# Expert rounds of a streaming encoder layer: three prompt blocks dense, two blocks by gathered rows, weights rounded on ScalarE

## The reference

```python
# per block of 128 tokens, 8 heads, 16 picks each
s1 = einsum('nhd,kd->nhk', q[:, :, 0], sub_keys_1); s2 = ... sub_keys_2
v1, i1 = top_k(s1, 16); v2, i2 = top_k(s2, 16)
sc, ci = top_k(v1[..., :, None] + v2[..., None, :], 16)      # over 256 sums
experts = e1 * 128 + e2;  gate = softmax(sc)
act = gelu(einsum('nhkd,nd->nhk', u_table[experts], xt))
out = einsum('nhk,nhkd->nd', gate * act, v_table[experts])
y = layer_norm(alpha * h + out)
```

## Time and profile before

| | |
|---|---|
| Time, median of 3 runs | 5350.22 us (5346.51 to 5352.82) |
| Profiled execution's own span | 5353.8 us |
| PE busy / PE weight loads | 94% / 82% |
| DVE / POOL / ACT busy | 54% / 53% / 11% |
| DMA: moved, mean rate | 830.40 MB, 155 GB/s |
| DMA rate in the late groups | about 205 GB/s |

### The profile page before, as it was taken

One profiled execution on the slowest core, in us unless ns is written; L12 is line 12 of the kernel. 1 busy time (PEld: TensorE's weight loads), 2 busy tenths in 40 slices (PEclk: granted clock), 3 DMA queues, 4 the chain that ended last, 5 costly groups with the idle time before them and its releaser, 6 DMA issues.

```text
span 5353.8 us, 73076 instructions
## 1 busy us (share of the span) xinstructions
PE 5036.4 (94%) x26783; PEld 4365.9 (82%) x26783; DVE 2896.3 (54%) x4592; ACT 611.3 (11%) x1293; POOL 2825.4 (53%) x1256
## 2 busy tenths in 40 slices
PE   8999999999999898888889999999999999999996
PEld 8999888787899798676677777778888888888884
DVE  1000343444332389788776666666665656565666
ACT  1000222222210110122100000000000000000002
POOL 4444222222444333422276777677777777777772
PEclk9999999999999999999899999999999999999998
DMA  5222233121432211233366666665555555555552
GB/s 186 95 103 104 105 117 117 65 78 67 143 118 87 73 55 63 80 135 137 146 213 231 235 226 229 226 223 196 202 212 205 206 205 208 196 212 203 204 201 97
DMA packets 214977, 830.40 MB, mean 155 GB/s; under 512 B 17009, under 2 KB 93937, under 8 KB 132721
## 3 DMA queue, kind: packets, MB, share of 16 engines
q1 hardware_dynamic: 53280, 388.00, 20.4%
q0 software_dynamic: 36864, 268.45, 13.2%
q10 hardware_dynamic: 124752, 173.08, 9.5%
HBM read 757.51 MB, written 77.33 MB: 156 GB/s over the span
## 4 chain that ended last, share of the span: by engine, by line
PE 79%; DVE 11%; issue 5%; DMA 3%; ACT 1%; POOL 1%; ACTq 0%; DVEq 0%; POOLq 0%
PE banks L356 26%; PE banks L541 24%; PE banks L605 21%; PE banks L587 2%; PE banks L425 2%; PE banks L387 1%; DMA work<-in_u_rows,idx 1%; PE banks L395 1%; DVE work L1166 1%; PE banks L510 1%; DVE work L1014 1%; DVE work L1122 1%; DVE work L1130 1%; DVE work L1162 1%; DVE ww_lo L1242 1%
## 5 line engine op out<-in xcount | busy, mean ns | idle before, releaser
L305 POOL TENSOR_SCALAR w_hi<-w_raw 128x2048 fp32r<-128x2048 f32 x370 | 710.3, 1920 | 2099.1 <-PE banks L356 1357.4
L307 POOL TENSOR_TENSOR w_lo<-w_raw,w_hi 128x2048 fp32r<-128x2048 f32 x370 | 1761.4, 4760 | 30.9
L356 PE MATMUL banks<-mv_hi,w_hi 128*128 128x320 f32 x3648 | 870.1, 320 | 60.0 <-DVE mv_lo L967 36.6
L605 PE MATMUL banks<-ww_hi,w_hi 128*128 128x512 f32 x2048 | 808.2, 395 | 50.5 <-DVE ww_lo L1242 35.8
L356 PE MATMUL banks<-mv_lo,w_hi 128*128 128x320 f32 x3648 | 841.0, 312 | 0.0
L356 PE MATMUL banks<-mv_hi,w_lo 128*128 128x320 f32 x3648 | 840.5, 312 | 0.0
L541 PE MATMUL banks<-mv_hi,w_hi 128*128 128x512 f32 x2048 | 818.7, 400 | 11.7 <-POOL w_lo L307 5.9
L541 PE MATMUL banks<-mv_hi,w_lo 128*128 128x512 f32 x2048 | 806.0, 394 | 0.0
L541 PE MATMUL banks<-mv_lo,w_hi 128*128 128x512 f32 x2048 | 805.2, 393 | 0.0
L605 PE MATMUL banks<-ww_lo,w_hi 128*128 128x512 f32 x2048 | 804.7, 393 | 0.0
L605 PE MATMUL banks<-ww_hi,w_lo 128*128 128x512 f32 x2048 | 804.4, 393 | 0.0
(11 more groups left out here) (140 smaller groups left out, 4292.5 us busy)
## 6 DMA issues: line engine op xcount, KB each, us to landing
w_raw<-in_wstream SPq DMA_DIRECT2D x370, 1024.0 KB, 4.8
gate_matrix<-work ACTq DMA_DIRECT2D x16, 2048.0 KB, 6.5
work<-gate_matrix ACTq DMA_DIRECT2D x32, 1024.0 KB, 6.1
out_p<-work ACTq DMA_DIRECT2D x34, 320.0 KB, 2.2
work<-out_p ACTq DMA_DIRECT2D x34, 320.0 KB, 3.4
gate_scratch<-work ACTq DMA_DIRECT2D x32, 320.0 KB, 2.2
work<-gate_scratch ACTq DMA_DIRECT2D x16, 640.0 KB, 4.0
early_act<-work ACTq DMA_DIRECT2D x24, 256.0 KB, 3.9
```

Of the source, the lines that this page charges most:

```text
L305: pool.tensor_scalar(w_hi[s][:, :], raw[s][:, :], 1.0, 0.0, ALU.mult, ALU.add).then_inc(hi_done, 1)
L307: pool.tensor_tensor(w_lo[s][:, :], raw[s][:, :], w_hi[s][:, :].bitcast(f32), ALU.subtract) \
L356: last = pe.matmul(acc(dst)[:, h, :], a[s][:, P * k:P * k + P], b[:, k, HALF * h:HALF * h + HALF], start=(k == k_first and n == 0), stop=( ...
L605: last = pe.matmul(banks[:, d, :], a[v % 2][:, at:at + P], b[:, e, :], start=(e == 0 and n == 0), stop=(e == EG - 1 and n == 2))
```

## The change

- The 128 sample tokens and the first prompt block now are the first 256 columns (`N1`), the other three prompt blocks the last 384 (`N2`). Every phase for 640 tokens runs its two waves as 256 and 384 columns, with separate tiles for the operands; copies and subtractions by ScalarE and VectorE are made in two instructions.
- Dense expert work covers 384 columns (12 blocks of 32 tokens in the gate matrix). The gather path covers two blocks, one after the other: 128 steps on u and 128 on v for each. Row buffers: four, in place of two. Indices are fetched eight at a time.
- 16 early expert units in place of 24 (4 ahead of the G loop, 3 of them beside the selection), 4 mixed trips in place of 6, with all 128 gathers of the first block's u (3, 3, 3, 3, 4, 2, 2, 1, 3, 3, 3, 2 by unit), and 24 late groups in place of 20, with two gathers a unit.
- From the third unit of the mixed trips on ScalarE rounds `w_hi` (`split_high`, behind `unit_done`), and POOL only subtracts (`split_low`, for the unit two ahead). POOL's order in iteration n: gathers of n, then `split_low` of unit n+2.
- Gelu of the late groups is done in the PSUM bank; product and remainder read PSUM.
- The gathered blocks are normalized in token layout on VectorE (`bn_stats`), the first in the middle of the late groups, and stored by POOL.

```diff
-STEPS_G = 2 * PICKS // GROUPS
-MIXED_STEPS = [[0], [1], [2], [3], [4, 5], [6], [7], [8, 9], [10], [11, 12], [13], [14, 15]]
+STEPS_M = PICKS // EARLY
+STEPS_G = 16
+ROWS = 4
+MIXED = [3, 3, 3, 3, 4, 2, 2, 1, 3, 3, 3, 2]
+LATE_STEPS = [[2 * n, 2 * n + 1] for n in range(2 * EG)]
...
+            def low(s):
+                pool.tensor_tensor(w_lo[s][:, :], raw[s][:, :], w_hi[s][:, :].bitcast(f32), ALU.subtract) \
+                    .then_inc(split_done, 1)
+            def split_low(s, pair):
+                pool.wait_ge(hi_late, 2 * pair + s + 1 - SELF_SPLIT)
+                low(s)
...
+            def gather(table, trip, per, c, skip):
+                pool.wait_ge(rows_used, per * trip + c + skip + 1)
...
+                if c % 8 == 4:
+                    fetch_idx(per * trip + c + 4, (c + 4) // 8 % 2)
+                pool.indirect_dma_start(rows_t[c % ROWS], None, table,
+                                        bass.IndirectOffsetOnAxis(ap=idx2[:, c % 16:c % 16 + 1], axis=0)) \
+                    .then_inc(rows_in[c % ROWS], 16)
...
             with pool.Fori(0, EARLY) as i:
                 for n in range(3 * EG):
-                    split_next(n % 2, (U_PEER + N_EARLY) // 2 + 6 * i + n // 2)
                     for c in MIXED_STEPS[n]:
-                        gather(u_rows, 2 * i + c // STEPS_G, c % STEPS_G)
...
+                        gather(u_rows, i, STEPS_M, c, 0)
+                    split_low(n % 2, SELF_SPLIT // 2 + 6 * i + n // 2)
+            def late_group(table, g, n_units, skip):
+                for n in range(2 * EG):
+                    for c in LATE_STEPS[n]:
+                        gather(table, g - late + PICKS // STEPS_G, STEPS_G, c, skip)
+                    if n < n_units:
+                        split_low(n % 2, (U_PEER + 2) // 2 + EG * g + n // 2)
...
+                        last = pe.matmul(acc(dst, h), a[s][:, P * k:P * k + P], b[h][:, k, :],
...
+            def split_high(s, pair):
+                act.wait_ge(raw_full[s], 16 * pair + 16)
+                act.activation(w_hi[s][:, :], raw[s][:, :], ACT.Copy).then_inc(hi_late, 1)
...
+            def act_units(g, q, first, pair):
                 load_gates(g, q)
                 for e in range(EG):
                     act.wait_ge(unit_done, first + e + 1)
+                    if e < EG - 1:
+                        split_high(e % 2, pair + e // 2)
+                    act.activation(banks[:, e, 0:N2], banks[:, e, 0:N2], ACT.Gelu).then_inc(gelu_done, 1)
+                    if e == EG - 1:
+                        split_high(e % 2, pair + e // 2)
+                    high_part(q, e, 0, banks[:, e, 0:N2])
+            def out_unit(first, pair, v):
+                act.wait_ge(unit_done, first + v + 1)
+                split_high(v % 2, pair + v // 2)
...
+            def act_units(g, q, steps):
                 dve.wait_ge(g4_in, 16 * q + 16)
                 for e in range(EG):
+                    bank = banks[:, e, 0:N2]
+                    steps(e, 0, 1)
                     dve.wait_ge(gelu_done, 4 * g + e + 1)
+                    product(bank, e)
+                    if e < EG - 1:
+                        steps(e, 1)
+                    low_part(q, e, 0, bank)
+                    if e == EG - 1:
+                        steps(e, 1)
...
+                for v in range(EG):
+                    steps(EG + v)
+                    add_out(g, v, U_PEER + 8 * g + EG, sums)
```

More of the change, by code:

```diff
@@ L24 @@
 T = SEQ + DEC_B * DEC_T
+N1 = 2 * P
+N2 = T - N1
+WAVES = ((0, N1), (N1, N2))
 HALF = T // 2
@@ L315, in _, with fetch_idx @@
                 split(s, 0)
-            with pool.Fori(1, (U_PEER + N_EARLY) // 2) as i:
+            with pool.Fori(1, SELF_SPLIT // 2) as i:
                 for s in range(2):
                     split_next(s, i)
-            def gather(table, g, c, first=0):
-                idx = idx2[:, c % 2:c % 2 + 1]
-                pool.wait_ge(rows_used, STEPS_G * g + c + 1)
+            def fetch_idx(at, half):
+                pool.tensor_copy(idx2[:, 8 * half:8 * half + 8], idx_all[:, ds(at, 8)]).then_inc(idx2_ready, 1)
@@ L555, in tail_units, with natural @@
                         act_step(n % 2, k, n % 2)
+            def natural(blk):
+                for k in range(KT_N):
+                    for n, part in enumerate((mv_hi, mv_lo)):
+                        last = pe.matmul(nat[:, P * k:P * k + P], part[0][:, k, P * blk:P * blk + P].bitcast(f32), ident,
+                                         start=(n == 0), stop=(n == 1))
+                last.then_inc(nat_ready, 1)
             tail_units(0, TAIL_PICKS)
@@ L589, in _, with out_units @@
                     last.then_inc(g_full, 1)
[L590 removed]
+            pe.wait_ge(g_evac, 2 + N2 // 4)
             pe.wait_ge(gelu_done, N_EARLY)
[L594 to L600 removed]
+            def out_units(q, first, z):
                 def part(v, d, e):
@@ new lines, in late_group, with act_n_gelu_pass @@
+            def late_group(g, n_units):
+                first, pair = U_PEER + 8 * g, (U_PEER + 2) // 2 + 4 * g
+                act_units(g, g, first, pair)
+                for v in range(n_units):
+                    out_unit(first + EG, pair + 2, v)
+            def act_n_gelu_pass():
+                act.activation(act_n, act_n, ACT.Gelu).then_inc(act_n_gelu, 1)
+            late = 2 * EARLY
+            act.wait_ge(act_n_ready, 1)
+            act_n_gelu_pass()
+            with act.Fori(late, late + PASS_G) as g:
+                late_group(g, EG)
@@ new lines, in _, with steps, early_product @@
+            with dve.Fori(0, EARLY) as i:
+                own.enter(i, 1)
+                q, first = 2 * i + 1, U_PEER + N_EARLY + 12 * i + EG
+                def steps(n, lo=0, hi=None):
+                    for c in MIXED_STEPS[n][lo:hi]:
+                        gather_step("u", i, STEPS_M, c, 0, STEPS_M * i)
+                def early_product(e):
+                    dve.wait_ge(act_in[e % 2], 16 * (2 * i + e // 2 + 1))
+                    product(act_t[e % 2], e)
+                act_units(EARLY + i, 2 * i, steps)
@@ L1307, in _, with late_group, steps @@
[L1307 to L1315 removed]
+            def late_group(table, g, skip, col, sums=False):
+                def steps(n, lo=0, hi=None):
+                    for c in LATE_STEPS[n][lo:hi]:
+                        gather_step(table, g - late + PICKS // STEPS_G, STEPS_G, c, skip, col)
+                act_units(g, g, steps)
+                for v in range(EG):
+                    steps(EG + v)
+                    add_out(g, v, U_PEER + 8 * g + EG, sums)
@@ new lines, in weights, with norm_stats @@
+            def weights(blk):
+                own.wait()
+                own.done(dve.tensor_scalar(nat, nat, ALPHA, None, ALU.mult))
+                own.wait()
+                dve.sem_inc(act_n_ready, 1)
+                dve.wait_ge(act_n_gelu, blk + 1)
+                own.done(dve.tensor_tensor(act_n, act_n, gate_n[blk], ALU.mult))
+                own.wait()
+            def norm_stats(blk, used):
+                dve.wait_ge(rows_used, used)
+                for c in range(4):
+                    last = dve.bn_stats(bn_s[:, c, :], nat[:, 512 * c:512 * c + 512])
+                own.done(last)
+                own.wait()
+                own.done(dve.bn_aggr(bn_mv, ln_n[:, 0:24]))
+                own.wait()
+                dve.tensor_scalar(rstd_n, bn_mv[:, 1:2], 1.0, EPS, ALU.mult, ALU.add).then_inc(n_var, 1)
@@ new lines, in norm_out @@
+            def norm_out(blk, trip):
+                dve.wait_ge(n_std, blk + 1)
+                own.done(dve.reciprocal(rstd_n, rstd_n))
+                own.wait()
+                dve.wait_ge(rows_in[0], 16 * trip + 16)
+                own.done(dve.scalar_tensor_tensor(rows_t[0], nat, bn_mv[:, 0:1], rows_t[0], ALU.subtract, ALU.mult))
+                own.wait()
+                dve.wait_ge(rows_in[1], 16 * trip + 16)
+                dve.scalar_tensor_tensor(rows_t[1], rows_t[0], rstd_n, rows_t[1], ALU.mult, ALU.add).then_inc(n_ready, 1)
@@ new lines, in _ @@
+            late = 2 * EARLY
+            weights(0)
+            with dve.Fori(late, late + PASS_G) as g:
+                late_group("v", g, 0, STEPS_G * (g - late))
+            norm_stats(0, 2 * PICKS + ROWS)
+            norm_out(0, 2 * PICKS // ROWS)
+            dve.wait_ge(rows_in[2], 16 * (2 * PICKS // ROWS) + 16)
+            own.done(dve.tensor_copy(nat, rows_t[2]))
+            own.wait()
+            dve.wait_ge(n_ready, 1)
+            dve.sem_inc(rows_used, ROWS)
+            with dve.Fori(late + PASS_G, late + 2 * PASS_G) as g:
+                own.enter(g - late - PASS_G, 1)
+                late_group("u", g, ROWS, STEPS_G * (g - late - PASS_G))
+                own.leave(PASS_G)
```

463 lines of the change are left out of this document (246 added, 217 removed).

## The result

The changed kernel takes 5671.01 us (median of four runs, 5666.55 to 5673.1) where the one before takes 5349.73: 1.0595 times as long, interval 1.058 to 1.061. The profiled execution has a span of 5671.3 us.

The account below looks back on a forecast made before the run. PE was taken as the bound, 79% of the chain. 2551 us to the mixed trips, 740 for these, 2352 for 24 late groups, 30 block change, 52 end: 5725 of span, so 5720 us, 7% slower; range 5400 to 6000.

Parts of the forecast that it names:

- The order: POOL's queue in the late part: gather(n) stands behind a subtraction waiting for unit n-1, issuing 6.9 us after its end.
- Terms of a late group: Late group: four expert units 33.2 us, a stall 6.0, two output pairs 58.0, clock 1; 98 us, against 87 before.
- The pairs: Late group: from output unit n-1 done to n+1 done takes 29.0 us, where PE alone needs 16.6.
- 72.7 + 3L: Late group's time in us, with L the first gather's landing, if the second lands by the first's DVE step.
- Mixed trip: Each of four trips: output half pairs 122 us, expert units 45, stall 6, DVE's early work 12; 185 us, before 139.
- The rest: Outside mixed trips and late groups: 2551 us before the trips, G loop 268 of it; block change 30; end 52.
- PE's gain: 256 dense units lose 2.54 us of matmul time each, 650 us, but no longer on the path.
- Instructions: Late part: ScalarE's weight rounding takes 1.95 us; products and low parts reading PSUM take 0.5 us each.
- Four buffers don't help: POOL reaches no gather earlier.: Late part: extra row buffers allow no earlier gather, since it stands behind the subtraction on POOL's queue; no size given.
- gathers land like weights: Gathers land in weights' 4.8 us median: 87.1 us a group, whole 5380 us; chance 0.04 (5340 to 5400).
- the gathers run ahead: Row waits leave the path and DMA bounds: late group 70 us, mixed trip 131, whole 4840; chance 0.08.
- Signs: After 2543 us PE busy about two thirds, waiting for adds, DVE for rows; 7 us from unit end to gather.

Follow-up runs that it names:

- the run with small rows: Changed kernel in its own order, each gather bringing 256 of a row's 2048 elements (128 KB for 1 MB): 5399.88 us.
- without rows: Changed kernel without all 512 gathers and the 512 VectorE steps on gathered rows, dense work kept in order: 4598.96 us.
- POOL's order alone: Changed kernel with gathers issued ahead of POOL's subtraction as far as row buffers are free: 5113.85 us, 0.9537 of the kernel before.
- the two orders together: Changed kernel with gathers issued ahead on POOL and, on DVE, output-unit adds ahead of row steps: 4832.23 us, 0.9014 of the kernel before.
- with the gates moved: Changed kernel with both queue orders on POOL and DVE, plus each group's gate load one output phase earlier: 4741.97 us, 0.8857 of the kernel before.

## Why the prediction was right

- **The order.** Right, and shown: 6.9 us from a unit's end to the next gather, as worked out; moving gathers or steps by one place takes 557 to 839 us away, with the same work.
- **Terms of a late group.** 98 us forecast, 97.0 in the first seven and 98.9 over all with the block change. The pairs hold as well. The end of the first output unit, that of the next group's first expert unit, and that of the next first output unit, by ScalarE's starts:

```profile
3498.51 1.91 ACT L963 ACTIVATE w_hi<-w_raw 128x2048 fp32r<-128x2048 f32 x1 [4.69 <-PE banks L650]
...
3556.74 1.92 ACT L963 ACTIVATE w_hi<-w_raw 128x2048 fp32r<-128x2048 f32 x1 [9.24 <-PE banks L587]
...
3596.48 1.91 ACT L963 ACTIVATE w_hi<-w_raw 128x2048 fp32r<-128x2048 f32 x1 [4.69 <-PE banks L650]
```

  The two pairs take 58.2 us here and 57.6 in the mean of six groups (58.0 forecast), the rest 39.8 and 39.4 (39.2).
- **Luck inside the group.** Two terms were off and cancel. PE's idle time is 22 us a group, where the stalls of the forecast add up to 30.8; the lower clock makes PE busy 9 us longer a group, where I added 1. In the turn shown PE may go on 19.6 us after the unit's end, for 20.7 forecast, and then its unit takes 11.1 for 8.3. The landing was too long from the start: 1.5 + 0.6 us and two MB at 370 GB/s are 7.8 for one gather beside one weight, not the 7.1 that I said they give again; measured are 7.3. So 72.7 + 3L, which has no term for the clock, gives 94.6 at 7.3, and the constant should be some 75. By the run with small rows the slope is 2.5 rather than 3.
- **Mixed trip.** 178.5 us for 185; four are 26 us less than the sum had.
- **The rest.** The G loop started at 2264.4, not 2275, and took 272 us for 268; it was 5 to the trips, for 8; DVE's end of the picks at 2234 stayed, the 10 us that I gave to doubled instructions of ScalarE and VectorE did not appear. From the last adds (5628.60) to the end are 43 us, for 52. The 54 us between 5725 and 5671 are 26 in the mixed trips and some 9 each ahead of them, in the late groups with the change of block, and at the end. All but the G loop came out shorter, and nothing tells why these terms leaned one way.
- **PE's gain.** 650 us of matmul time did go: without rows the time is 4599, with PE gapless at 66.2 us a group (66.3 forecast).
- **Instructions.** Rounding 1.910 us (1.95); the 384-column products and low parts about 0.55 (0.5).
- **"Four buffers don't help: POOL reaches no gather earlier."** Too strong: holding the late groups to what two allow costs 73 us in this order. The forecast didn't need it, since my pairs of units let a gather go without a wait for a buffer.
- **The pages' figures.** The estimate of 4.4 us for a gather from the Trainium skill, "DMA: Bandwidth & Descriptors", section "Anatomy of one DMA — SWDGE (gpsimd) path", is still not met: no gather of the changed kernel landed under 5.4 us. Even 128 KB took 2.7 us at best and 4.5 in the median, where the page's formula makes an estimate of 2.3. My reading of its 358 GB/s was wrong: the same page of the Trainium skill, in section "Bandwidth", gives about 358 GB/s as each core's part when both cores of an HBM domain stream, and up to 425 for one core alone. Here one core runs, so neither the 379 GB/s of the earlier trace rows nor the 387 above speaks against it.
- **Rival "gathers land like weights"**, 5380: its price was right in kind (the run with small rows, landing at 4.5 us, took 5400), its condition did not hold.
- **Rival "the gathers run ahead"**, 4840: both conditions that I gave for it were too weak. POOL's order alone meets the second (a gather passed before unit n-1 is done) and took 5114; the small rows meet the first (L of 4.5 or less) in their median and took 5400. That the two orders together took 4832 is partly chance, for what held that kernel was the late gates and the mixed trips. Nor was 70 us a group the floor: with the gates moved it is 67.0, at 387 GB/s where I took 370.
- **Signs.** PE was busy 65% of the mixed trips and 78% of the late groups, for "about two thirds"; who waited for whom was as said.

## What to carry to other kernels

Before a stream is thickened, write down for each item where its issue stands in its queue, what the instruction ahead of it waits for, and how far its use is; buffers help only as far as that distance lets them. If a change removes work from the bounding engine and the time rises, look in the waits for a circle through the queues, and move one link by one place: here that turned 1.06 of the time before into 0.90, and moving the next late load into 0.886. Then count again what stands behind each wait: one place too far cost 121 us.

## What the runs showed that was not expected

- The DMA engines kept 387 GB/s for 469 us on end, with gathers and weight loads mixed, while gathers landed in 9.0 us in the median: rate and landing time rise together, and the latter costs nothing where the distance is there.
- A gather of 128 KB lands only 2.8 us earlier than one of 1 MB (4.5 and 7.3 us, beside a traffic of 125 and 268 GB/s): by these two more than half of the landing time is not the bytes, as an estimate.
- A late group, with four or five stalls of PE, runs at 0.88 of the clock, without rows at 1.00 (the windows above): part of a stall's price is paid after it, at half the matmul rate for 4 us behind one of 6.5.
